# Order of the attention stage: both score chunks, values, transposes of head 0, then the sample slots

## The reference, cut to what matters

```
x += W_out[ norm_a(DilatedMix(q_a,k_a,v_a)) || norm_b(SlidingWindow(q_b,k_b,v_b)) ]
x += SwiGLU(rmsnorm(x))
```

## Time and profile before

| what | us |
|---|---|
| median of 3 runs (3111.5 to 3117.1) | 3116.52 |
| the profiled execution, its own time | 3107.87 |
| its span, first to last instruction | 3106.3 |
| attention stage of layer 0 (324.6 to 628.0) | 303.4 |
| attention stage of layer 1 (1853.8 to 2157.3) | 303.5 |
| PE busy in each of these two | 280.6, 280.7 |

### The profile page before, as it was taken

How to read it: one execution, slowest core, us unless ns; L and a number is a source line. 1 busy time by engine, 2 the same in 40 slices (tenths; PEclk the granted TensorE clock), 3 DMA queues, 4 the chain that set the end, 5 groups by cost and what they waited for, 6 DMA issues and landing times.

```text
span 3106.3 us, 52475 instructions
## 1 busy us (share of the span) xinstructions
PE 2876.3 (93%) x19546; PEld 2659.6 (86%) x19546; DVE 1196.1 (39%) x2524; ACT 828.0 (27%) x1612; POOL 509.3 (16%) x211
## 2 busy tenths in 40 slices
PE   4999999977899999999969999997869999999998
PEld 4999666567899999999969996665859999999998
DVE  5444555452432222223254445554442222233223
ACT  2111566521221111112031126664122111112110
POOL 1222000022122122112122210001121221112110
PEclk6999999988899999999989999998879999999999
DMA  4121443124444445411021124521244455551111
GB/s 156 43 62 48 140 125 100 51 97 150 138 163 163 150 150 177 150 41 41 14 92 48 55 65 137 146 77 39 97 150 151 150 177 182 187 183 62 41 41 56
DMA packets 182634, 333.36 MB, mean 107 GB/s; under 512 B 30480, under 2 KB 142096, under 8 KB 179664
## 3 DMA queue, kind: packets, MB, share of 16 engines
q1 hardware_dynamic: 171632, 195.20, 20.2%
q0 software_dynamic: 2816, 135.99, 13.0%
q10 hardware_dynamic: 8032, 0.17, 0.2%
HBM read 309.08 MB, written 157.94 MB: 150 GB/s over the span
## 4 chain that ended last, share of the span: by engine, by line
PE 87%; DVE 5%; DMA 3%; issue 3%; ACT 2%; POOL 0%; ACTq 0%; DVEq 0%; SPq 0%; POOLq 0%
PE ps L404 66%; PE ps L1436 3%; PE ps L1450 3%; PE ps L1425 3%; DMA f_raw<-in_w_gate_up_dram 2%; PE ps L1346 2%; DVE g_lo L958 1%; PE ps L1499 1%; DVE hf L943 1%; PE ps L1356 1%; DVE hf L953 1%; PE ps L1487 1%; PE ps L1468 1%; DVE t_buf L943 1%; PE ps L1311 1%
## 5 line engine op out<-in xcount | busy, mean ns | idle before, releaser
L404 PE MATMUL ps<-g_hi,f_hi 128*128 128x352 f32 x2496 | 814.6, 326 | 35.1 <-DVE g_lo L958 35.0
L404 PE MATMUL ps<-g_hi,f_lo 128*128 128x352 f32 x2496 | 810.0, 325 | 0.0
L404 PE MATMUL ps<-g_lo,f_hi 128*128 128x352 f32 x2496 | 808.8, 324 | 0.0
L404 PEld LDWEIGHTS ps<-g_hi,f_hi 128*128 128x128 f32 x2496 | 473.7, 190 | 42.4 <-DVE g_lo L958 42.4
L630 POOL TENSOR_TENSOR f_lo<-f_raw,f_hi 128x2048 fp32r<-128x2048 f32 x66 | 303.6, 4611 | 1229.5 <-ACT f_hi L875 1229.5
L404 PEld LDWEIGHTS ps<-g_hi,f_lo 128*128 128x128 f32 x2496 | 474.7, 190 | 0.0
L404 PEld LDWEIGHTS ps<-g_lo,f_hi 128*128 128x128 f32 x2496 | 474.5, 190 | 0.0
L1269 DVE TENSOR_TENSOR silu<-silu,ps 128x352 f32<-128x352 f32 x132 | 68.8, 521 | 821.4 <-ACT silu L897 821.4
L1279 DVE TENSOR_TENSOR xm<-xm,ps 128x352 f32<-128x352 f32 x528 | 271.1, 520 | 199.4 <-PE ps L404 199.4
L404 PE MATMUL ps<-a_hi,f_hi 128*128 128x352 f32 x1056 | 340.6, 323 | 0.0
L404 PE MATMUL ps<-a_hi,f_lo 128*128 128x352 f32 x1056 | 338.4, 320 | 0.0
(11 more groups left out here) (166 smaller groups left out, 3396.3 us busy)
## 6 DMA issues: line engine op xcount, KB each, us to landing
out_dram<-in_cache_a_dram POOLq DMA_DIRECT2D x16, 8176.0 KB, 27.3
f_raw<-in_w_gate_up_dram SPq DMA_DIRECT2D x44, 1024.0 KB, 31.3
f_raw<-in_w_down_dram SPq DMA_DIRECT2D x22, 1024.0 KB, 4.9
k_near<-in_cache_a_dram SPq DMA_DIRECT2D x16, 1024.0 KB
v_near<-in_cache_a_dram SPq DMA_DIRECT2D x16, 1024.0 KB
w_raw<-in_w_in_dram SPq DMA_DIRECT2D x28, 512.0 KB, 3.9
k_far<-in_cache_a_dram SPq DMA_DIRECT2D x16, 768.0 KB
v_far<-in_cache_a_dram SPq DMA_DIRECT2D x16, 768.0 KB
```

Source lines behind the costliest of these rows:

```text
L404: mm = pe.matmul(out, left(a, c), right(b, c), start=(start and c == 0 and k == 0), stop=(stop and c == n - 1 and k == 2))
```

## The change

The places A and B are kept and `FILL` is the same, but on PE and DVE they now stand together, behind the second score chunk, the values and (on PE) the transposes of head 0. On ACT, `keep_probs(d, 0)` moves ahead of the slots A, while `softmax(d+1, 1)` stays between A and B.

```diff
 ACT:
                     if 0 <= d + 1 < ND:
                         softmax(d + 1, 0)
+                    if 0 <= d < ND:
+                        keep_probs(d, 0)
                     for _ in range(FILL[2 * (d + 2)]):
                         next(beside)
-                    if 0 <= d < ND:
-                        keep_probs(d, 0)
                     if 0 <= d + 1 < ND:
                         softmax(d + 1, 1)
 DVE:
+                    if d + 2 < ND and len(key_tiles[d + 2]) > 4:
+                        mask_and_min(d + 2, 1)
+                    if d >= 1:
+                        keep_mix(d - 1)
                     for _ in range(FILL[2 * (d + 2)]):
                         next(beside)
-                    if d >= 1:
-                        keep_mix(d - 1)
-                    if d + 2 < ND and len(key_tiles[d + 2]) > 4:
-                        mask_and_min(d + 2, 1)
                     for _ in range(FILL[2 * (d + 2) + 1]):
                         next(beside)
 PE:
+                    if d + 2 < ND and len(key_tiles[d + 2]) > 4:
+                        score(d + 2, 1)
+                    if d >= 1:
+                        mix(d - 1)
+                    if 0 <= d < ND:
+                        turn_probs(d, 0)
                     for _ in range(FILL[2 * (d + 2)]):
                         next(beside)
-                    if d >= 1:
-                        mix(d - 1)
-                    if d + 2 < ND and len(key_tiles[d + 2]) > 4:
-                        score(d + 2, 1)
-                    if 0 <= d < ND:
-                        turn_probs(d, 0)
                     for _ in range(FILL[2 * (d + 2) + 1]):
                         next(beside)
```

## The result

The changed kernel is slower: 3195.11 us median (3191.68 to 3201.12, 4 runs), beside 3115.06 of the kernel before in the same comparison. The ratio is 1.026, 95% interval 1.0241 to 1.028. The direction is the forecast one, the size is not: +80 us where +44.6 was forecast, outside the range of 3137 to 3184. The profiled execution took 3193.39, 85.5 more than that of before.

What follows compares the result with a forecast made beforehand. TensorE was taken as the bound, so only its idle time counts. Terms of 16.0 + 5.5 + 2.4 + 1.9 + 1.8 + 0.5 - 1.8 - 4.0 gave 22.3 us a layer, +44.6 in all: 3161 us, range 3137 to 3184.

Steps and rivals of the forecast that it cites:

- What bounds the kernel: Whole kernel: TensorE, 87% of the chain; reordering only changes its idle time, 22.8 us per attention layer.
- Part 1: Second score chunk directly behind the first: fourth chunk waits for DVE's mask to free its bank, 16 x 1.00 us a layer.
- Part 2, the exponentials: `mix` loses slots A as cover while ACT does each sequence's sample exponentials: +5.5 us a layer, bounds 0 and 12.
- Part 3, "the rest of the covers for `mix` ... +0.5": Mixer b steps: the copy for `mix` must fit under one 256-wide score pair; +0.5 us a layer, bounds 0 and 3.
- Part 3, the clock: Lower granted clock behind the two new `rows_s` waits, counted once: +1.8 us a layer, bounds 0 and 3.5.
- Part 3, runs of slots: Longer slot runs wait for earlier slots' reading, +2.4 us a layer; two new output-slot waits for `rows_s`, +1.9.
- part 4: Spread slots' waits for `inv_p` partly go, at steps 28 and 56; a new one at 42: -1.8 us a layer.
- Part 5: Slots A followed by transposes or slots instead of `mix` are cheaper: -4.0 us a layer, or -8.8 by the tiling-mode drain rule.
- (a): Rival: the first chunk's mask is not late, so the second chunk's bank wait costs nothing; 3129 us, chance 0.10.
- (b): Rival: one wait pays for others, ACT and DVE catching up during TensorE's bank wait; -4.8 us a layer, 3107, chance 0.07.
- (c): Rival: idle gaps, every second bank wait of the second chunk, lower the clock; 27 us more, 3188, chance 0.10.
- The signs: Changed profile: `min_first` wait 5 to 10 us a layer, `mix` 12 to 15, five `rows_s` waits, stage 320 to 330.

Runs made afterwards that it cites:

- part 1 alone: Kernel before with only the second score chunk and its DVE mask moved ahead of slots A: 3144.58 us, ratio 1.010.
- the change without part 1: Changed kernel with the second score chunk and its mask back behind the values and head 0's transposes, still ahead of the slots: 3187.50 us, ratio 1.0237.
- lost cover without the long run: Kernel before with slots A behind the values and second score chunk, ahead of head 0's transposes; slots B and ACT as before: 3183.54 us, ratio 1.0227.
- the long run with cover: Changed kernel, slots still in one run, but head 0's transposes first, then second score chunk, then values: 3155.44 us, ratio 1.0124.
- the version that beats before: Kernel before, slots kept at A and B, but behind slots A: head 0's transposes, second score chunk, then values: 3091.10 us, ratio 0.9935.

## Why the prediction was right in direction and wrong in size

For a layer 22.3 us were forecast, and 40.9 and 44.0 came. The profiles split the loss. In the table, each column is the difference to the kernel before, in us, for both attention stages together. The clock column is an estimate: half of what the time at the lower level grew, as if TensorE had worked through it at half speed. The rest is other busy time. A profile is one execution and can lie some us off the median.

| version | longer | idle | clock | rest |
|---|---|---|---|---|
| changed kernel | 84.9 | 46.9 | 20.5 | 17.5 |
| part 1 alone | 37.1 | 10.1 | 8.5 | 18.4 |
| the change without part 1 | 79.3 | 53.2 | 23.9 | 2.2 |
| lost cover without the long run | 80.8 | 44.3 | 37.5 | -1.0 |
| the long run with cover | 46.7 | 17.6 | 15.4 | 13.8 |
| the version that beats before | -20.9 | -18.9 | -3.4 | 1.4 |

- **What bounds the kernel: right.** The whole difference is in the attention stages. They got longer with unchanged work, by TensorE's waits and its clock.
- **Part 1, +16.0 a layer: right alone.** 2.06 from first to fourth chunk, 7.1 idle, +32 us in both layers. In the changed kernel, however, it adds only 5 to 8 us to the slots-only version. The third chunk still costs its time alone (the rest is 15.3 us larger), but idle time and clock are together 9.7 smaller. It fits that ACT is less late where TensorE waits for the bank.
- **Part 2, the exponentials, +5.5: near.** In the changed kernel the six long waits of the values of steps 10, 15, 30, 44, 45 and 51 are 1.48, 1.83, 1.10, 1.48, 1.20 and 1.61. The same steps waited 1.47, 0.64, 0.12, 1.47, 0.12 and 0.34 before: +4.5. Step 15 was forecast at 2.1. The wait of step 59, 0.98 before, is gone (forecast -0.7), which leaves +3.5.
- **Part 3, "the rest of the covers for `mix` ... +0.5": the first of the two terms that failed.** The other 33 waits of the values make 10.9 us; before, the waits outside those seven steps made 4.2: +6.7, and there is more in the scores ahead of them, whose last 0.07 no longer overlaps with anything. A typical one, step 25 in order of time:

```profile
445.63 0.70 PE L1425 MATMUL ps<-kt_all,xm 64*128 64x256 f32 x4
445.69 0.77 ACT L763 ACTIVATE pt<-ps 128x512 f32<-128x512 f32 x2 [0.24 <-PE ps L1436]
...
446.60 0.66 PE L1450 MATMUL ps<-pt,v_all 128*64 128x128 f32 x8 [0.26 <-ACT pt L763]
```

The 0.77 copy with its signals does not fit under one 256-wide score pair of 0.70. The earlier trace rows had both numbers, and I took the fit for granted; 0.97 instead of 0.63 behind the score is 0.34, and the values wait in 26 of the 32 steps of mixer b, where they did in 7. The run with the lost cover only shows how much hangs on the covers: +71 us, with 29.6 us of values' waits in layer 0.
- **Part 3, the clock, +1.8: the other term that failed, and the larger miss.** I had the two low periods of before and one more; layer 0 has seven and layer 1 nine. With 30.7 and 37 us of low time instead of 14, at half speed, this is about 8.5 and 12 us a layer. The sum took the wait of step 14 as its case. Behind the same wait of 0.96 in step 56 the kernel before had a low period three times as long, 10.2 us:

```profile
574.00:587.00 13.00, 9.89 (x62) 7.34 (x64) 2.93 (x11) 3.50 (x10) 0.00 (x0) 0.61 0.50 148
```

Filling the waits of the output slots took the low time back to about that of before (24 us in both layers, before 27).
- **Part 3, runs of slots (+2.4, +1.9) and part 4 (-1.8): near.** `near` waits 4.4 us in all, the output slots +2.0 as forecast, `inv_p` -1.2.
- **Part 5, -4.0: seen in part.** The `near` and `far` pieces got 2.6 cheaper, from start to start without waits. That each of the 55 steps saves 0.16 (-8.8) no run here shows.
- **Rivals.** (a) is refuted by the 2.06. Its argument that TensorE signals each head by itself does not help: in the trace of before the last records of the two heads of a 512-wide pair start 0.53 and 0.54 after the first. (b) is half right: one wait does pay for others, but it hides part of a loss that is larger than the one I had. Of (c), the clock does fall, but mostly behind the output slots. The waits of the second chunk have a smaller share: part 1 alone has 17 and 27 us of low time where before had 14, about 8.5 us for both layers and not the 27 of (c).
- **The signs.** The bank's 2.06, the five output slots and `inv_p` below 5.0 came as named. The values wait 19.6 where 12 to 15 was named, the stages are 344 and 348 us long where 320 to 330 was, and TensorE's busy time is not the same.

What stays open: why the parts do not add (32, 71 and 75 alone, 80 together), and why some waits are followed by the lower clock and others of the same length are not. Of the covered long run the table gives idle time, clock and rest, but no run separates what of the rest is the third chunk and what are transposes made dearer by what follows them.

## What to carry to other kernels

Work that fills the gap between producing something for a slower engine and consuming it is cover. Once it is away, each step pays what the copy takes beyond the rest of the gap: before moving it, compare copy plus signals with what is left in the gap, at the commonest step and not at the worst one. Two waits of one engine for different partners need not add, since each can give the other partner time; a part tried alone can cost nearly as much as the whole. And a gap can be closed by placing independent work of the step ahead of the consumer, as here the transposes and the second chunk ahead of the values.

## What the runs showed of the hardware that was not expected

- The two heads' score matmuls, on different halves of the rows, run side by side, the last record of head 0 starting 0.53 and that of head 1 0.54 after the pair's start. So DVE starts on head 0 only 1.31 after a 512-wide pair starts, though each matmul signals by itself.
- A wait of about 0.96 us between the values slot and the output slot was followed within 4 us by the lower clock, for 3.4 to 10.2 us, in all ten places of the changed kernel and in four of six of the kernel before. Eight unread transposes in that gap took the low time of the kernel before from 13.7 to 6.8 us a layer and made it 8 us faster, their own cost included.
